# Both products of the delta rule's 64-wide join over all 128 rows, with zeros in the idle half of one factor

## The chip, the cores and the metric

One NeuronCore of a Trainium2 chip runs the kernel. The metric is the device time in microseconds of one execution; the time before the change is the median of three runs.

## The reference

One decoder layer on 256 tokens of width 2048, in float32. The input is projected to the operands of two token mixers, a gated delta rule with 16 heads of 128 and a differential softmax attention with 16 heads; their outputs are gated, merged and projected, and a dense SwiGLU layer follows. What matters here is the delta rule. Each head works in chunks of 64 tokens:

```
k_beta = k * beta
a_mat = jnp.where(strict, jnp.einsum('bhncd,bhnsd->bhncs', k_beta, k) * decay, 0.0)
sol = lax.linalg.triangular_solve(a_mat + jnp.eye(C, dtype=f32), rhs, left_side=True,
                                  lower=True, unit_diagonal=True)
```

The kernel does not solve this way. It treats 128 tokens at a time as one unit, two chunks of 64 with the passage between them kept in the same 128 by 128 matrix, builds the inverse of the unit lower triangle, and multiplies by it.

## The kernel before, in words

**The work.** Everything hangs on one stream of weight tiles of 256 by 512 (in DRAM in the order of use), each 512 KB. SyncE's queue brings them into a ring of four (`raw`), ScalarE rounds a tile to fp32r (`whi`), VectorE forms the remainder (`wlo`), both three tiles ahead of use, and TensorE takes twelve matmuls of 512 columns per tile: for two blocks of 128 rows of the weights and two of 128 tokens, activation high part by weight high part, high by low, low by high. The result gathers in the PSUM buffers `pg`.

**The slots.** The first five bodies are of 32 slots each, one weight tile per slot (`BODY`, `TPG`). Each engine's program walks the slots and calls, after the tile of a slot, functions with an `if s == ...` that put in a piece of the mixers. So the order of the small work within each engine is written out by hand, by slot numbers, and engines meet through counting semaphores. In body j (0 to 3) `dn_conv` and `dn_build` prepare four heads of the delta rule; `dn_scan` in body j + 1 uses what they built.

**The build.** For the four heads there are eight units of 128 tokens (index i, 0 to 7). `AT` holds for each the scaled and masked matrix of key products, 128 by 128. The inverse is built from blocks of 8 (on GpSimd) to 16 to 32 (slots 19 to 23), then the 32-wide blocks are joined to 64 (slots 25 to 27), and the 64-wide ones to 128 in the last slots, called the join here. `T` holds the inverse of the upper 64 rows (its rows 64 to 127 are cleared once at the start and not written again), and `TTf` the whole inverse, transposed, as it grows.

**The join.** In slot 29 (`OFF_64`) TensorE computes for each unit the product of `AT[0:64, i, 64:128]` with `T[0:64, i, :]` (L648 to 651). The results of units 0 to 3 go to PSUM partitions 64 to 127, those of units 4 to 7 to partitions 0 to 63, alternately. ScalarE copies them to `Pm`, units 0 to 3 to its rows from 64 and units 4 to 7 to its rows from 0 (L1058, L1059), and beforehand it has copied the lower right block of `TTf` for units 4 to 7 to rows 0 to 63 (L1056), since both factors of a product must lie in the same rows. In slot 30 TensorE computes the second product for each unit, units 0 to 3 over rows 64 to 127 and units 4 to 7 over rows 0 to 63 (L655 to 658), and ScalarE copies the negated results into the upper right block of `TTf` (L1062, L1063). The reader of the finished `TTf` is the first product of `dn_scan` in slot 1 of the next body (L673).

**Around it.** `S` holds the state of the delta rule after the first half of the tokens. ScalarE writes it in slot 2 of a body (L1106), TensorE reads it in slot 3 (`pe_ks`, L686 to 690), and it is unused until the next body. GpSimd, in each body, steps the blocks of 8, issues four transfers of the first turn (`blocks_in`, L1415), finds the reciprocal root for the key norms and signals `pool_rinv` (L1437, L1438), and then issues the four transfers of the second turn and the four of the values. `dn_scan` on VectorE waits for `pool_rinv` in slot 0 of the next body.

A product in fp32 (`float32` operands) shows as two LDWEIGHTS and two MATMULs in the profile; one of fp32r operands as one of each. `B8`, `B4` and `C8` are views of the PSUM buffers `B`.

Of the kernel before, what the change touches and what calls it, by code (L numbers as in the profile page):

```python
# [106 lines left out]
def build(nc, xT, xrow, weights, w_ab, consts, early, params, lam_in, ln_in, out):  # L107
# [8 lines left out]
    with ctx:  # L116
# [80 lines left out]
        B4 = [b[:, :].rearrange("p (h d) -> p h d", h=HB) for b in B]  # L197
        B8 = [b[:, :].rearrange("p (h d) -> p h d", h=8) for b in B]
        C8 = [b[:, 0:8 * SB].rearrange("p (h d) -> p h d", h=8) for b in B]
        TT, WT = Pm[:, :, 0:SB], Pm[:, :, SB:CH]  # L200
        sel = masks[:, 0, 0:SB // EB]
        eye32 = masks[:, 6, :]
# [34 lines left out]
        def d_(name):  # L237
            a, b = DS[name]
            return dsm[:, a:b]
# [254 lines left out]
        def _(pe):  # L494
            def mm(o, l, r, start=True, stop=True):
                return nc.tensor.matmul(o, l, r, start=start, stop=stop)  # L496
# [110 lines left out]
            def dn_build(j, s):  # L607

                if s == 13:
                    pe.wait_ge(N["act_silu"], 1 + 3 * j + 1)  # L610
                    pe.wait_ge(N["dve_conv"], 1 + 6 * j + 2)
                    pe.wait_ge(N["dve_o1"], 1 + j)
                    for t in range(TOK):
                        for h in range(HB):
                            kc = cT[:, 0, h, t * P:(t + 1) * P]
                            last = mm(B4[2 + t][:, h, :], kc, kc)
                    last.then_inc(N["pe_kk"], 1)
                if s in GROW:
                    k = GROW[s]
                    f0, f1 = SB if k == 0 else 0, SB if k == GROWN - 1 else CH  # L620
                    pe.wait_ge(N["dve_x"], 1 + GROWN * j + k + 1)
                    waits_end()
                    for i in range(8):
                        for q in range(4):
                            a = sub(q)
                            last = mm(B8[1][a, i, f0:f1], (Tc if k == 0 else Pc)[a, i, :], Pm[a, i, f0:f1])
                    last.then_inc(N["pe_x"], 1)
                if s == OFF_P:
                    pe.wait_ge(N["dve_t"], 1 + 2 * j + 1)
                    pe.wait_ge(N["act_at"], 1 + j + 1)  # L630
                    waits_end()
                    for i in range(8):
                        for q in (0, 2):
                            last = mm(C8[2][sub(q + 1), i, :], AT[sub(q), i, sub(q + 1)], Tc[sub(q), i, :])
                    last.then_inc(N["pe_p"], 1)
                if s == OFF_T:
                    pe.wait_ge(N["dve_p"], 1 + j + 1)
                    waits_end()
                    for i in range(8):
                        for q in (0, 2):  # L640
                            b = sub(q + 1)
                            last = mm(C8[1][sub(q), i, :], Pc[b, i, :], TT[b, i, :])
                    last.then_inc(N["pe_t"], 1)
                if s == OFF_64:
                    pe.wait_ge(N["dve_t"], 1 + 2 * (j + 1))
                    pe.wait_ge(N["act_tt"], 1 + j + 1)
                    waits_end()
                    for i in range(HB):  # L648
                        mm(B8[1][CH:P, i, :], AT[0:CH, i, CH:P], T[0:CH, i, :])
                        last = mm(B8[1][0:CH, HB + i, :], AT[0:CH, HB + i, CH:P], T[0:CH, HB + i, :])  # L650
                    last.then_inc(N["pe_p21"], 1)
                if s == OFF_64 + 1:
                    pe.wait_ge(N["act_p21"], 1 + j + 1)
                    waits_end()
                    for i in range(HB):  # L655
                        mm(B8[2][0:CH, i, :], Pm[CH:P, i, :], TTf[CH:P, i, CH:P])
                        last = mm(B8[1][0:CH, i, :], Pm[0:CH, HB + i, :], Pm[0:CH, i, :])
                    last.then_inc(N["pe_x21"], 1)

            def dn_scan(j, s, alone=False):  # L660
# [207 lines left out]
        def _(act):  # L868
            def copy(o, i, scale=1.0):
                return nc.scalar.activation(o, i, ACT.Copy, scale=scale)  # L870
# [153 lines left out]
            def dn_build(j, s):  # L1024
                if s == 2 and not isinstance(j, int):
                    sums_in(j)
                if s in DECAY and not isinstance(j, int):
                    past(j, s - DECAY[0], len(DECAY))
                    if s == DECAY[-1]:
                        decay(j)  # L1030
                if s == 12 and isinstance(j, int):
                    past(j, 0, 1)
                if s == 13 and isinstance(j, int):
                    decay(j)
                if s in AT_SCALED:
                    a = 4 * AT_SCALED.index(s)
                    act.wait_ge(N["dve_ss"], 1 + j + 1)
                    for i in range(a, a + 4):
                        last = nc.scalar.activation(AT[:, i, :], AT[:, i, :], ACT.Copy, scale=d_("e")[:, i:i + 1])
                    if a:  # L1040
                        last.then_inc(N["act_at"], 1)
                if s == 24:
                    silu(j, 1)
                if s == OFF_COPY:
                    act.wait_ge(N["dve_t"], 1 + 2 * j + 1)
                    for q in range(4):
                        a = slice(q * SB, (q + 1) * SB)
                        copy(TTf[a, :, a], TT[a])
                    for q in range(2):
                        a = slice(q * SB, (q + 1) * SB)  # L1050
                        last = copy(T[a, :, a], Tc[a])
                    last.then_inc(N["act_tt"], 1)
                if s == OFF_64:
                    act.wait_ge(N["dve_t"], 1 + 2 * (j + 1))
                    act.wait_ge(N["act_tt"], 1 + j + 1)
                    copy(Pm[0:CH, 0:HB, :], TTf[CH:P, HB:8, CH:P])  # L1056
                    act.wait_ge(N["pe_p21"], 1 + j + 1)
                    copy(Pm[CH:P, 0:HB, :], B8[1][CH:P, 0:HB, :])  # L1058
                    copy(Pm[0:CH, HB:8, :], B8[1][0:CH, HB:8, :]).then_inc(N["act_p21"], 1)  # L1059
                if s == OFF_64 + 1:  # L1060
                    act.wait_ge(N["pe_x21"], 1 + j + 1)
                    copy(TTf[0:CH, 0:HB, CH:P], B8[2][0:CH, 0:HB, :], -1.0)  # L1062
                    copy(TTf[0:CH, HB:8, CH:P], B8[1][0:CH, 0:HB, :], -1.0).then_inc(N["act_x21"], 1)  # L1063

            def blocks_out(scratch, kept):

# [327 lines left out]
        def _(pool):  # L1394
# [5 lines left out]
            def root(o, x):  # L1400

                a = half[:, 0:x.shape[1]]
                for i in range(3):
                    ch(G.tensor_tensor(a, o, o, ALU.mult))  # L1404
                    ch(G.tensor_tensor(a, a, x, ALU.mult))
                    ch(G.tensor_scalar(a, a, -0.5, 1.5, ALU.mult, ALU.add))  # L1406
                    last = G.tensor_tensor(o, a, o, ALU.mult)
                    if i < 2:
                        ch(last)
                return last  # L1410
# [7 lines left out]
            for j in range(NB + 1):  # L1418
                if j > 0:
                    pool.wait_ge(N["dve_qs"], 1 + j)  # L1420
                    root(d_("rs"), d_("qs")).then_inc(N["pool_rs"], 1)
                if j < NB:
                    pool.wait_ge(N["dve_a8"], 1 + j + 1)
                    for k in range(EB - 1):
                        col, row, part, rest = below(k)
                        ch(G.tensor_tensor(part, col, row, ALU.mult))  # L1426
                        last = G.tensor_tensor(rest, rest, part, ALU.subtract)  # L1427
                        if k < EB - 2:
                            ch(last)
                    last.then_inc(N["pool_t8"], 1)  # L1430
                    for i in range(2):
                        pool.wait_ge(c_kept, 16 * (2 * j + i + 1))
                        pool.wait_ge(N["dve_raw"], 1 + 2 * j + i)
                        blocks_in(turn_c, moved, c_full)
                        if i == 0:
                            pool.wait_ge(N["dve_ss"], 1 + j + 1)
                            ch(root(d_("rk"), d_("ss")))  # L1437
                            G.tensor_tensor(d_("rinv"), d_("rk"), d_("ss"), ALU.mult).then_inc(N["pool_rinv"], 1)  # L1438
                    pool.wait_ge(v_kept, 16 * (j + 1))
                    pool.wait_ge(N["dve_ktail"], 1 + j + 1)  # L1440
                    blocks_in(turn_v, vtok, v_full)
# [847 lines left out]
```

## Time and profile before the change

| what | value |
| --- | --- |
| median of 3 runs | 1893.19 us (1892.96 to 1893.9) |
| the profiled execution | 1893.05 us |
| its span, first to last instruction | 1891.0 us |
| mean granted TensorE clock | 0.998 of full |
| TensorE busy | 1875.3 us, 99% |
| VectorE, ScalarE, GpSimd busy | 1322.6, 919.5, 200.4 us |
| DMA | 389.70 MB, 206 GB/s on average |

The profile is of one execution. Times of its rows count from the start of the span. A timeline row gives the start, the time from the first start to the last end, the engine, the line of the kernel, the operation, the tiles written and read, the rows and columns of the stationary factor ("64\*64"), the shape and type streamed, and how many instructions were merged into the row; PEld is TensorE's weight load, which overlaps its matmuls.

### The profile page before, as it was taken

How to read it: one execution, taken by the hardware profiler on the slowest of the kernel's cores; microseconds unless marked ns; L12 is line 12 of the kernel's file. 1: busy time of each engine (PE TensorE's matmuls, PEld its weight loads, DVE VectorE, ACT ScalarE, POOL GpSimd, SP SyncE). 2: the span in 40 equal slices, each digit the busy share in tenths (PEclk: the TensorE clock that was granted, in tenths of full speed). 3: DMA queues.
4: the chain of work that ended last, by engine and by line, in shares of the span. 5: the costliest groups of instructions: out<-in, count | busy, mean ns of one | idle time of the engine just before them, and what ended most of it. 6: DMA issues, size and time to landing. Idle time of an engine off the chain costs nothing.

```text
span 1891.0 us, 29975 instructions
## 1 busy us (share of the span) xinstructions
PE 1875.3 (99%) x9647; PEld 1548.5 (82%) x9647; DVE 1322.6 (70%) x1859; ACT 919.5 (49%) x1234; POOL 200.4 (11%) x480
## 2 busy tenths in 40 slices
PE   9999999999999999999999999999999999999997
PEld 7788888878888888888888888888888888888886
DVE  7888889897666767675577657577765466654656
ACT  5655565664454545556444437444443444443442
POOL 0303022030023232333000000000000000000000
PEclk9999999999999999999999999999999999999999
DMA  7667667584567676766666775556655566665565
GB/s 273 214 200 221 213 209 226 184 250 159 190 197 245 215 243 218 246 214 212 200 197 192 231 244 168 200 189 196 192 193 197 190 192 196 191 197 191 190 191 176
DMA packets 117970, 389.70 MB, mean 206 GB/s; under 512 B 14512, under 2 KB 23536, under 8 KB 117744
## 3 DMA queue, kind: packets, MB, share of 16 engines
q1 hardware_dynamic: 97904, 351.65, 57.8%
q10 hardware_dynamic: 14592, 24.14, 4.0%
q0 software_dynamic: 5376, 12.59, 2.5%
q8 instruction: 63, 1.03, 0.2%
q14 instruction: 35, 0.29, 0.0%
HBM read 368.91 MB, written 19.42 MB: 205 GB/s over the span
## 4 chain that ended last, share of the span: by engine, by line
PE 96%; DVE 1%; DMA 1%; POOL 0%; issue 0%; ACT 0%; SPq 0%; DVEq 0%; ACTq 0%; POOLq 0%
PE pg L496 91%; PE B L496 5%; DVE gates L1474 1%; DMA raw<-in_weights 0%; POOL Tc L1427 0%; DMA qT<-turn_c 0%; PE B L596 0%; POOL Tc L1426 0%; PE B L816 0%; ACT whi L870 0%; DVE act_b L1466 0%; DVE wlo L1466 0%; POOL qT L1415 0%; PE B L744 0%; DVE lnst L2170 0%
## 5 line engine op out<-in xcount | busy, mean ns | idle before, releaser
L1466 DVE TENSOR_TENSOR wlo<-raw,whi 128x1024 fp32r<-128x1024 f32 (+1 forms) x640 | 778.5, 1219 | 468.0 <-ACT whi L870 448.9
L870 ACT ACTIVATE whi<-raw 128x1024 fp32r<-128x1024 f32 (+1 forms) x640 | 673.8, 1057 | 747.7 <-PE pg L496 715.7
L496 PE MATMUL pg<-whi,act_x 128*128 128x512 f32 x2960 | 936.0, 393 | 1.8 <-ACT whi L870 1.8
L496 PEld LDWEIGHTS pg<-whi,act_x 128*128 128x128 f32 x2960 | 555.3, 188 | 120.5 <-ACT whi L870 2.2
L496 PE MATMUL pg<-wlo,act_x 128*128 128x512 f32 x1480 | 574.6, 390 | 0.0
L496 PE MATMUL pg<-whi,act_a 128*128 128x512 f32 x1632 | 504.6, 389 | 0.0
L496 PEld LDWEIGHTS pg<-whi,act_a 128*128 128x128 f32 x1632 | 306.3, 188 | 63.8 <-DVE act_a L1466 0.2
L496 PEld LDWEIGHTS pg<-wlo,act_x 128*128 128x128 f32 x1480 | 278.1, 188 | 55.0
L496 PE MATMUL pg<-wlo,act_a 128*128 128x512 f32 x816 | 317.5, 389 | 0.0
L496 PEld LDWEIGHTS pg<-wlo,act_a 128*128 128x128 f32 x816 | 153.2, 188 | 31.7
L496 PE MATMUL pg<-whi,act_b 128*128 128x512 f32 x512 | 158.5, 389 | 0.0
L496 PEld LDWEIGHTS pg<-whi,act_b 128*128 128x128 f32 x512 | 96.1, 188 | 19.9
L496 PE MATMUL pg<-wlo,act_b 128*128 128x512 f32 x256 | 99.6, 389 | 0.0
L1931 DVE STREAM_TRANSPOSE soft<-hraw 32x256 f32<-32x256 f32 x208 | 90.6, 436 | 3.8
L496 PEld LDWEIGHTS pg<-wlo,act_b 128*128 128x128 f32 x256 | 48.0, 188 | 10.0
L1474 DVE SCALAR_TENSOR_TENSOR cT<-vda,cw,cT 128x255 f32<-128x255 f32 (+2 forms) x96 | 41.8, 477 | 1.1
L1177 ACT ACTIVATE soft<-soft,sm 128x128 f32<-128x128 f32 (+1 forms) x64 | 28.3, 445 | 15.3 <-DVE sm L1470 15.3
L1415 POOL DMA_DIRECT2D gates<-turn_p x48 | 26.1, 550 | 38.0 <-DMA turn_p<-gates 38.0
L1426 POOL TENSOR_TENSOR Tc<-Tc 128x7 f32<-128x7 f32 (+3 forms) x28 | 16.1, 576 | 130.6 <-DVE Tc L1664 128.7
L1406 POOL TENSOR_SCALAR half<-half 128x2 f32<-128x2 f32 (+1 forms) x72 | 24.3, 337 | 6.4
L1474 DVE SCALAR_TENSOR_TENSOR soft<-cst,sm,B 128x384 f32<-128x384 f32 x32 | 18.2, 609 | 9.0 <-PE B L496 7.6
L1404 POOL TENSOR_TENSOR half<-dsm 128x8 f32<-128x8 f32 x24 | 6.3, 263 | 168.7 <-DVE dsm L1471 167.4
(265 smaller groups left out, 1086.6 us busy)
## 6 DMA issues: line engine op xcount, KB each, us to landing
raw<-in_weights SPq DMA_DIRECT2D x646, 512.0 KB, 4.2
turn_c<-hraw ACTq DMA_DIRECT2D x8, 512.0 KB, 3.2
qT<-turn_c POOLq DMA_DIRECT2D x32, 128.0 KB, 3.3
turn_q<-hraw ACTq DMA_DIRECT2D x6, 512.0 KB, 3.7
gates<-turn_q ACTq DMA_DIRECT2D x24, 128.0 KB, 5.0
turn_p<-gates POOLq DMA_DIRECT2D x12, 192.0 KB, 3.8
gates<-turn_p POOLq DMA_DIRECT2D x48, 48.0 KB, 4.0
decm<-sums_out ACTq DMA_DIRECT2D x4, 512.0 KB, 3.6
```

Source lines behind the costliest of these rows:

```text
L496: return nc.tensor.matmul(o, l, r, start=start, stop=stop)
L870: return nc.scalar.activation(o, i, ACT.Copy, scale=scale)
L1177: last = nc.scalar.activation(pr[:, m, a:b], pr[:, m, a:b], ACT.Exp, bias=sm[:, 28 + i:29 + i], accum_out=sm[:, 32 + i:33 + i])
L1404: ch(G.tensor_tensor(a, o, o, ALU.mult))
L1406: ch(G.tensor_scalar(a, a, -0.5, 1.5, ALU.mult, ALU.add))
L1415: pool.dma_start(dst[b * SB:(b + 1) * SB], scratch[:, :, b].rearrange("a x (q i) -> x a q i", i=SB)).then_inc(full, 16)
L1426: ch(G.tensor_tensor(part, col, row, ALU.mult))
L1466: return V.tensor_tensor(o, a, b, op)
L1474: return V.scalar_tensor_tensor(out=o, in0=a, scalar=s, in1=b, op0=op0, op1=op1)
L1931: ins = V.transpose(blocks_out(turned)[b * SB:(b + 1) * SB, :, :, a, :], blocks_in[a * SB:(a + 1) * SB, :, :, b, :])
```

## The change

All eight products of each place run over rows 0 to 127. In the first, both factors are taken whole: rows 64 to 127 of `T` are zero. All results land in PSUM partitions 64 to 127. ScalarE copies them in one instruction to rows 64 to 127 of `joined`, a view of `S` as eight blocks of 64; rows 0 to 63 of it are cleared by GpSimd in every body, in front of the operation that signals `pool_rinv`, once the readers of `S` are done. In the second product `joined` with its zero rows is multiplied by all rows of the right half of `TTf`, the results land in partitions 0 to 63, and one ScalarE copy negates them into `TTf`. The copy of the lower right block to `Pm` is gone, and ScalarE waits for `pool_rinv` before it writes `joined`.

```diff
@@ -197,6 +197,7 @@
         C8 = [b[:, 0:8 * SB].rearrange("p (h d) -> p h d", h=8) for b in B]
+        joined = S[:, :, :].rearrange("p h (e d) -> p (h e) d", d=CH)
@@ -645,16 +646,14 @@
                     pe.wait_ge(N["dve_t"], 1 + 2 * (j + 1))
                     pe.wait_ge(N["act_tt"], 1 + j + 1)
                     waits_end()
-                    for i in range(HB):
-                        mm(B8[1][CH:P, i, :], AT[0:CH, i, CH:P], T[0:CH, i, :])
-                        last = mm(B8[1][0:CH, HB + i, :], AT[0:CH, HB + i, CH:P], T[0:CH, HB + i, :])
+                    for i in range(8):
+                        last = mm(B8[1][CH:P, i, :], AT[:, i, CH:P], T[:, i, :])
                     last.then_inc(N["pe_p21"], 1)
                 if s == OFF_64 + 1:
                     pe.wait_ge(N["act_p21"], 1 + j + 1)
                     waits_end()
-                    for i in range(HB):
-                        mm(B8[2][0:CH, i, :], Pm[CH:P, i, :], TTf[CH:P, i, CH:P])
-                        last = mm(B8[1][0:CH, i, :], Pm[0:CH, HB + i, :], Pm[0:CH, i, :])
+                    for i in range(8):
+                        last = mm(B8[2][0:CH, i, :], joined[:, i, :], TTf[:, i, CH:P])
                     last.then_inc(N["pe_x21"], 1)
@@ -1053,14 +1052,12 @@
                 if s == OFF_64:
                     act.wait_ge(N["dve_t"], 1 + 2 * (j + 1))
                     act.wait_ge(N["act_tt"], 1 + j + 1)
-                    copy(Pm[0:CH, 0:HB, :], TTf[CH:P, HB:8, CH:P])
+                    act.wait_ge(N["pool_rinv"], 1 + j + 1)
                     act.wait_ge(N["pe_p21"], 1 + j + 1)
-                    copy(Pm[CH:P, 0:HB, :], B8[1][CH:P, 0:HB, :])
-                    copy(Pm[0:CH, HB:8, :], B8[1][0:CH, HB:8, :]).then_inc(N["act_p21"], 1)
+                    copy(joined[CH:P, :, :], B8[1][CH:P, :, :]).then_inc(N["act_p21"], 1)
                 if s == OFF_64 + 1:
                     act.wait_ge(N["pe_x21"], 1 + j + 1)
-                    copy(TTf[0:CH, 0:HB, CH:P], B8[2][0:CH, 0:HB, :], -1.0)
-                    copy(TTf[0:CH, HB:8, CH:P], B8[1][0:CH, 0:HB, :], -1.0).then_inc(N["act_x21"], 1)
+                    copy(TTf[0:CH, :, CH:P], B8[2][0:CH, :, :], -1.0).then_inc(N["act_x21"], 1)
@@ -1435,6 +1432,9 @@
                             pool.wait_ge(N["dve_ss"], 1 + j + 1)
                             ch(root(d_("rk"), d_("ss")))
+                            if j:
+                                pool.wait_ge(N["pe_ks"], 1 + j)
+                            ch(G.memset(S[0:CH, :, :], 0.0))
                             G.tensor_tensor(d_("rinv"), d_("rk"), d_("ss"), ALU.mult).then_inc(N["pool_rinv"], 1)
```

## Rows read from the trace of the kernel before

**Rows 1.** The page, busy time of each engine with its share and instructions.

```profile
PE 1875.3 (99%) x9647; PEld 1548.5 (82%) x9647; DVE 1322.6 (70%) x1859; ACT 919.5 (49%) x1234; POOL 200.4 (11%) x480
```

**Rows 2.** The page, the chain that ended last, by engine.

```profile
PE 96%; DVE 1%; DMA 1%; POOL 0%; issue 0%; ACT 0%; SPq 0%; DVEq 0%; ACTq 0%; POOLq 0%
```

**Rows 3.** Waits of TensorE from 40 to 500 us: total, times, longest.

```profile
PE B L496 <- DVE Pc L1466: 1.2, 1, 1.2
```

**Rows 4.** Timeline of TensorE around an fp32 product of 128 by 128, first body on.

```profile
117.74 0.39 PE L496 MATMUL pg<-whi,act_x 128*128 128x512 f32 x1
117.96 1.05 PE L496 MATMUL B<-vr,TTf 128*128 128x128 f32 x8
118.77 0.48 PE L496 MATMUL pg<-whi,act_x 128*128 128x512 f32 x1
119.09 0.40 PE L496 MATMUL pg<-wlo,act_x 128*128 128x512 f32 x1
```

**Rows 5.** Timeline of TensorE around the first join product, first body.

```profile
103.38 0.39 PE L496 MATMUL pg<-whi,act_x 128*128 128x512 f32 x1
103.69 0.68 PE L496 MATMUL B<-T,AT 64*64 64x64 f32 x16
104.31 0.50 PE L496 MATMUL pg<-whi,act_x 128*128 128x512 f32 x1
104.64 0.39 PE L496 MATMUL pg<-wlo,act_x 128*128 128x512 f32 x1
```

**Rows 6.** Timeline of TensorE around the second join product, first body.

```profile
106.94 0.39 PE L496 MATMUL pg<-whi,act_x 128*128 128x512 f32 x1
107.25 0.27 PE L496 MATMUL B<-TTf,Pm 64*64 64x64 f32 x1
107.26 0.27 PE L496 MATMUL B<-Pm 64*64 64x64 f32 x1
107.36 0.22 PE L496 MATMUL B<-TTf,Pm 64*64 64x64 f32 x1
...
107.71 0.22 PE L496 MATMUL B<-TTf,Pm 64*64 64x64 f32 x1
107.72 0.22 PE L496 MATMUL B<-Pm 64*64 64x64 f32 x1
107.87 0.50 PE L496 MATMUL pg<-whi,act_x 128*128 128x512 f32 x1
```

**Rows 7.** Timeline of the weight loads there, first and last of one tile's eight.

```profile
107.25 0.13 PEld L496 LDWEIGHTS B<-TTf,Pm 64*64 64x64 f32 x1 [0.35 <-issue]
...
107.66 0.14 PEld L496 LDWEIGHTS B<-TTf,Pm 64*64 64x64 f32 x1
```

**Rows 8.** Timeline of TensorE at the attention's score products.

```profile
523.36 0.39 PE L496 MATMUL pg<-whi,act_x 128*128 128x512 f32 x1
523.67 1.58 PE L496 MATMUL B<-kT,qT 64*128 64x128 f32 x16
```

**Rows 9.** Timeline of TensorE at the second half of the beta and a projections.

```profile
23.08 0.39 PE L496 MATMUL pg<-whi,act_x 128*128 128x512 f32 x1
23.30 1.99 PE L496 MATMUL B<-act_x,act_a 128*64 128x256 f32 x16
25.12 0.40 PE L496 MATMUL pg<-whi,act_x 128*128 128x512 f32 x1
```

**Rows 10.** Timeline of ScalarE around the join, first body.

```profile
104.14 0.41 ACT L870 ACTIVATE Pm<-TTf 64x256 f32<-64x256 f32 x1
104.57 0.77 ACT L870 ACTIVATE Pm<-B 64x256 f32<-64x256 f32 x2
105.37 1.06 ACT L870 ACTIVATE whi<-raw 128x1024 fp32r<-128x1024 f32 x1
```

**Rows 11.** Timeline of GpSimd, first body.

```profile
81.40 0.20 POOL L1438 TENSOR_TENSOR dsm<-dsm 128x8 f32<-128x8 f32 x1
89.81 2.21 POOL L1415 DMA_DIRECT2D qT<-turn_c  x4 [8.21 <-DMA turn_c<-hraw]
```

**Rows 12.** Instructions that touch the tile T: VectorE's clear, ns min/median/max.

```profile
L1498 DVE MEMSET T<- x1: 485/485/485, 2.0 to 2.0; 128x512 f32 x1
```

## The prediction

> **What bounds the kernel now.** I read the page first. TensorE is busy for 99% of the span and ends 96% of the chain of waits [rows 1, 2]; no other engine passes 70%. So time added to TensorE's own stream is added to the run, and time saved on ScalarE is worth nothing unless TensorE waits for it. Inside the delta rule TensorE's waits have one entry for VectorE that matters below: 1.2 us, once, for the operand of a growth step in the first body [rows 3].
>
> Next the timeline of TensorE around the two places that the change touches. Between two weight products of 512 columns the start-to-start gap is 0.22 to 0.23 us (117.74 to 117.96 in [rows 4]). The first join product is 16 recorded matmuls (each fp32 product shows as two): the last wide product before it starts at 103.38, the first small one at 103.69, the next wide ones at 104.31 and 104.64 [rows 5]. From wide start to the second wide start behind it that is 1.26 us, of which two ordinary gaps (0.46) would be there anyway. The parts are 0.31 in, 0.46 from first to last small start (0.68 less the 0.22 that the last one lasts), 0.15 out, 0.33 to the next. The second product is the same: 106.94 is its wide start and 107.87 the next, and here the trace lists the matmuls one by one [rows 6]. The reader is to see that they start in pairs 0.01 us apart, one from each of the two 64-row, 64-column tiles, and that a tile starts its next only 0.058 us later ((107.71-107.36)/6), the first step being 0.11. The loads of one tile keep the same step: (107.66-107.25)/7 = 0.059 us [rows 7]. So the 0.46 us for 16 is not 0.03 each: it is eight steps of a tile, with two tiles side by side.
>
> **The change, part by part.** There are four bodies and two places in each, so everything on TensorE counts eight times.
>
> Number of instructions: eight products per place before, eight after; 16 recorded loads and 16 matmuls either way. Loaded columns (64) and moving columns (64) do not change.
>
> What changes is the side by side. All eight products of a place now use all 128 rows and write the same 64 output partitions, so there is one tile and nobody to pair with. Sixteen steps of one tile: 0.11 + 14 x 0.058 = 0.92 us from first to last start, against 0.46. That the longer column of rows costs nothing by itself is seen in the wide fp32 products: 8 matmuls, 128 rows, take 1.05 us, so (1.05-0.27)/7 = 0.111 each for 128 loaded columns [rows 4], almost exactly twice the 0.058 for 64. The step follows the columns, not the rows. I take 0.058; the lower bound is the 0.031 per matmul of today's pairs (0.46/15), the upper one is in the second rival.
>
> Entry and exit. The products of 128 by 128 are entered after 0.22 us and left after 118.77 - 118.74 = 0.03, then 0.32 [rows 4]. The 64 by 64 ones pay 0.31, 0.15 and 0.33 [rows 5], and so do the score products of 64 rows by 128 columns, 0.31 on entry [rows 8]. The difference, 0.09 + 0.12 + 0.01 = 0.22 us, is paid for each detour out of the full array. Does a product of 128 rows by 64 columns pay it? One stage has that shape, the beta and a projections: entry 0.22, exit 25.12 - 25.01 = 0.11, which is its own step of (1.99-0.28)/15 = 0.114, so nothing is paid [rows 9]. But that stage multiplies fp32r operands into partitions from 0, as one matmul per product; the join is fp32 at two matmuls per product, and its first product goes to partitions from 64. Every fp32 stage with fewer than 128 rows pays; no fp32 one with 64 columns and 128 rows exists here. So one row is nearest by shape and the others by type and by how many matmuls a product takes. I take the detour as still paid (0.22 us kept), because the small fp32 tiles pay it in both shapes shown; the other end is 0.22 us gained per place. The Trainium skill, "TensorEngine Tiling (Array Packing)", sections Available Configurations and Key Properties, lists 128 by 64 as a mode of its own and says that a change of mode drains the engine: by that rule the detour stays and the sum is the one below; by the projection rows alone it would be the first rival's.
>
> Per place: +0.46 us. Eight places: +3.7 us.
>
> ScalarE loses a copy at the first place (0.41 us) and replaces two of 64 by 256 (0.77 us together) with one of 64 by 512 [rows 10]; two of half its width take 0.77 together, so one takes no more. I cost it at nothing: the copy behind the first product ended at 105.34 and the second product starts at 107.25, a cover of 1.9 us, and a first product that ends 0.46 us later still leaves 1.4 us. Without that cover each 0.1 us would be four tenths over the run. Behind the ScalarE waits stands the rounding of the next weight tile at 105.37; it starts some 0.3 us later (0.46 later product, less what the single copy saves), and TensorE wants that tile only three tiles on, at 12 x 0.23 = 2.7 us each, with VectorE's subtraction between. The new wait of ScalarE for the pool's inverse is met long before: the pool finishes it at 81.6 in the first body [rows 11] and ScalarE asks at 104. The result copy at the second place ends 0.4 us later; its reader comes at 117.96 [rows 4].
>
> GpSimd clears 64 rows of S in front of that inverse and waits for the state products of the body before, which lie at its beginning, over 50 us back. Queued behind the clear are the inverse and the four transfers of the second turn, issued from 89.81; between 81.6 and 89.81 the pool is idle [rows 11], 8.2 us of cover. No row shows a pool clear of this size. VectorE's clear of T, 512 elements per partition, took 0.485 us [rows 12]; I take the pool's as 0.5 to 1.0 us, hidden. What it could do is hold up VectorE in the first body, where TensorE is already waiting for VectorE [rows 3]: nothing at the low end, its own length of 1.0 us once at the high end. I take 0, since it starts at about 81.4, when the product whose result that growth step needs is not yet being worked on by VectorE.
>
> **The sum.** The profiled execution took 1893.05 us for a span of 1891.0. 1893.05 + 8 x 0.46 = 1896.73; it stands 0.14 below the median of the three runs, so against that the forecast is 1893.19 + 3.7 = 1896.9 us.
>
> **The rivals.** *No detour:* the 128-row shape is run as part of the full array. Then 0.22 + 15 x 0.058 + 0.03 + 0.32 = 1.44 us per place against 1.26, +0.18, times eight +1.45: 1894.6 us. For it the projection rows [rows 9]; against it that they are of another type and go to the lower partitions. Chance 0.18.
>
> *Load and stream in turn:* with one set of rows in use, a load can't run under the matmul before. The step is then 0.058 for the load plus 0.055 for the stream (128 streamed columns fit into a step of 0.111 [rows 4], so 64 take at most half), 0.113 us; 15 x 0.113 - 0.46 = +1.24 per place, +9.9 in all: 1903.1 us, slower beyond doubt. It decides as soon as the step passes 0.059. Against it: the wide fp32 products hide a 128-column load under a 128-column stream on the same rows, at 0.111. The Trainium skill, "TensorE: Matmul & The Clock Gate", section Part 3, has this rule (a load overlaps a running matmul only where the row group differs); the wide rows speak against it. Chance 0.07.
>
> *Not slower at all:* the full array takes the products with neither detour nor loss of the side by side, at 0.031 per matmul: 0.22 + 0.46 + 0.03 + 0.32 = 1.03 us per place, -0.23, in all -1.8: 1891.4 us. It decides if the 0.058 step belongs to the two-tile mode and not to 64 loaded columns; against it stands 0.111 for 128. Chance 0.05.
>
> **How the numbers follow.** The forecast case has 0.70. A measurement of this kernel can tell about 0.2%, 3.8 us, from no change, and +3.7 lies just under that: half of this case falls on either side, and the pool's clear can only push it up. So slower by over 0.2% is 0.35 + 0.07 = 0.42, within 0.2% is 0.35 + 0.18 + 0.03 = 0.56, faster 0.02. The range goes down to the first rival less a few tenths (1894.2) and up to the forecast with 1.0 us for the clear and some tenths of step (1898.6); in-turn loading and the gain are left out.
>
> **What would show it.** In the changed profile both places list 16 matmuls of 128 by 64 columns in about 1.14 us (0.92 + 0.22) where 0.68 stood, 0.31 after the last wide start, and the next wide one 0.15 after the last small start. The first rival shows 0.22 and 0.03 to 0.11 there; the second about 1.95 us for the sixteen. A TensorE wait over 1.2 us in the first body would be the clear's. Wrong I would be most simply if the step of one tile with 128 rows is not 0.058.

## The result, and the profile after

The changed kernel takes 1897.32 us (median of 20 runs), the kernel before, run beside it, 1893.82 us (20 runs): 3.5 us more. The ratio is 1.0017, 95% interval 1.0011 to 1.0024, so +2.1 to +4.5 us. One run of the kernel before took 2349.5 us, far over 1.5% above its fastest, and is left out of the ratio as a slow one. The forecast was +3.7 us, 1896.9 us.

The page after, the lines that answer to [rows 1, 2]: busy times, and the chain that ended last.

```profile
PE 1880.0 (99%) x9647; PEld 1553.2 (82%) x9647; DVE 1322.9 (70%) x1859; ACT 916.9 (48%) x1222; POOL 203.2 (11%) x484
...
PE 95%; DVE 2%; DMA 1%; ACT 1%; issue 1%; POOL 0%; SPq 0%; DVEq 0%; ACTq 0%; POOLq 0%
```

The same number of matmuls and loads (9647 each) keeps TensorE busy 4.7 us longer. ScalarE has 12 instructions fewer and 2.6 us less to do, which bought nothing: TensorE still sets the end.

The timeline of TensorE around the first place, first body, the answer to [rows 5]:

```profile
103.82 0.39 PE L497 MATMUL pg<-whi,act_x 128*128 128x512 f32 x1
104.14 1.15 PE L497 MATMUL B<-T,AT 128*64 128x64 f32 x16
105.21 0.50 PE L497 MATMUL pg<-whi,act_x 128*128 128x512 f32 x1
105.55 0.39 PE L497 MATMUL pg<-wlo,act_x 128*128 128x512 f32 x1
```

and around the second, the answer to [rows 6]; here all sixteen are one form and stand in one row:

```profile
107.84 0.39 PE L497 MATMUL pg<-whi,act_x 128*128 128x512 f32 x1
108.16 1.15 PE L497 MATMUL B<-TTf,S 128*64 128x64 f32 x16
109.23 0.50 PE L497 MATMUL pg<-whi,act_x 128*128 128x512 f32 x1
109.57 0.39 PE L497 MATMUL pg<-wlo,act_x 128*128 128x512 f32 x1
```

The sixteen matmuls take 1.15 us where they took 0.68. Entry is 104.14 - 103.82 = 0.32, the next gap 0.34: as before within 0.01. From wide start to second wide start it is 105.55 - 103.82 = 1.73 us against 1.26, and 109.57 - 107.84 = 1.73 at the second place. The other three bodies show the same gaps within 0.01. In the trace's single records the difference is 0.46 at each place: 8 x 0.46 = 3.7 us.

The weight loads of the first place, the answer to [rows 7]:

```profile
104.14 1.01 PEld L497 LDWEIGHTS B<-T,AT 128*64 128x64 f32 x16 [0.35 <-issue]
```

Sixteen loads start over about 0.87 us (1.01 less the 0.14 that one lasts), 0.058 apart, while each matmul is recorded as lasting 0.22. So each load is recorded under matmuls of the same rows. The ends of matmuls are modelled in this profile; a reading that rests on starts alone stands at the full array below.

ScalarE and GpSimd, from their timelines, the answers to [rows 10, 11]:

```profile
105.40 0.60 ACT L869 ACTIVATE S<-B 64x512 f32<-64x512 f32 x1 [0.82 <-PE B L497]
106.02 1.06 ACT L869 ACTIVATE whi<-raw 128x1024 fp32r<-128x1024 f32 x1
```

```profile
80.65 0.52 POOL L1437 MEMSET S<- 64x512 f32 x1
81.25 0.20 POOL L1438 TENSOR_TENSOR dsm<-dsm 128x8 f32<-128x8 f32 x1
90.28 2.22 POOL L1412 DMA_DIRECT2D qT<-turn_c  x4 [8.82 <-DMA turn_c<-hraw]
```

The copy ends at 106.00 and the second product starts at 108.16, 2.2 us of cover. The clear takes 0.52 us and the pool is idle for 8.8 us behind it.

The two profiled executions lie 1897.35 - 1893.05 = 4.3 us apart, 0.6 more than the eight places. Matched weight product by weight product, the two traces move apart by 0.46 us at each of the eight places, 3.70 in all, and otherwise in four stretches only: the changed kernel is 0.73 us ahead after the first 21 us, then loses 0.87 where TensorE stopped once, 0.30 at the wait for the growth step [rows 3], and 0.2 near 1161 us. So the 0.6 is a sum of several differences of these two executions, and one of them alone, the stop, is larger than it. The stop lies in the middle of a growth step of the first body, among products that all stand behind one and the same wait. In its timeline:

```profile
78.82 0.97 PE L497 MATMUL B<-Pm,Pc 32*32 32x64 f32 x52
80.37 0.41 PE L497 MATMUL B<-Pm,Pc 32*32 32x64 f32 x12 [0.58 <-issue]
```

The executions profiled of four of the variants below (two column tiles, no clear, first place only, by twos) do not have this gap, and it is not in the profile of the kernel before. What caused it no run shows.

### The profile page after: what moved, and what is told of

It is laid out like the page before. It is cut to its first block, busy times and chain, and to the rows that moved or that the text cites. A ratio compares the mean times of both kernels' runs of the same rounds, so it can differ in the third digit from the quotient of the medians.

```text
span 1895.3 us, 29974 instructions
## 1 busy us (share of the span) xinstructions
PE 1880.0 (99%) x9647; PEld 1553.2 (82%) x9647; DVE 1322.9 (70%) x1859; ACT 916.9 (48%) x1222; POOL 203.2 (11%) x484
## 4 chain that ended last, share of the span: by engine, by line
PE 95%; DVE 2%; DMA 1%; ACT 1%; issue 1%; POOL 0%; SPq 0%; DVEq 0%; ACTq 0%; POOLq 0%
PE pg L497 90%; PE B L497 5%; DVE gates L1474 1%; DMA raw<-in_weights 1%; ACT whi L869 0%; DMA qT<-turn_c 0%; POOL Tc L1424 0%; DVE wlo L1466 0%; DVE act_b L1466 0%; PE B L597 0%; POOL Tc L1423 0%; DVE sm L1474 0%; ACT gates L1295 0%; POOL qT L1412 0%; PE B L815 0%
## 5 line engine op out<-in xcount | busy, mean ns | idle before, releaser
L997 ACT ACTIVATE cT<-vda,cw 128x256 f32<-128x256 f32 x32 | 14.4, 497 | 21.4 <-DVE vda L1602 21.4
```

The lines of the kernel that those rows point to most:

```text
L997: last = nc.scalar.activation(cT[:, kind, h, :], conv_in(kind, h), ACT.Copy, scale=cw[:, kind, h, CONV - 1:CONV])
```

## The experiments

All are compared with the kernel before on the same chip. A "place" is one of the two products of the join; its length is taken from the wide start ahead of it to the second wide start behind it: 1.26 us before, 1.73 after.

**Two column tiles over 128 rows.** The changed kernel, with the units split over both halves of the output partitions:

```diff
-                    for i in range(8):
-                        last = mm(B8[1][CH:P, i, :], AT[:, i, CH:P], T[:, i, :])
+                    for i in range(HB):
+                        mm(B8[1][CH:P, i, :], AT[:, i, CH:P], T[:, i, :])
+                        last = mm(B8[1][0:CH, HB + i, :], AT[:, HB + i, CH:P], T[:, HB + i, :])
```

and the same at the second place.

> The changed kernel, all products still over 128 rows, but units 0 to 3 and 4 to 7 write opposite halves of the output partitions, alternately, in both places; the ScalarE copies are two of 64x256 again. Theory (what was lost is the side by side of two tiles, rows cost nothing): each place goes from 1.15 us for its 16 matmuls back to about 0.68, entry 0.31 and exit 0.15 stay; 8 x 0.46 = 3.7 us less than the changed kernel, the time of the kernel before within 0.5 us. Rival (128 rows exclude any pairing, both column halves wait for the same row streams): the 16 stay at 1.15 us and the kernel at +3.5 us over before.

Measured 1893.71 us against 1893.84, ratio 0.9997 (0.9988 to 1.0006). Its first place in the timeline of TensorE:

```profile
104.09 0.39 PE L497 MATMUL pg<-whi,act_x 128*128 128x512 f32 x1
104.41 0.69 PE L497 MATMUL B<-T,AT 128*64 128x64 f32 x16
105.02 0.50 PE L497 MATMUL pg<-whi,act_x 128*128 128x512 f32 x1
105.36 0.39 PE L497 MATMUL pg<-wlo,act_x 128*128 128x512 f32 x1
```

These are 128 rows, zeros and all, and the place takes 1.27 us as in the kernel before. The whole loss is in how many tiles the products are spread over; the rows, the clear and the state buffer cost nothing that can be seen. The rival falls.

**First place in the full array.** The changed kernel, with all 128 columns of `AT` loaded and 128 output partitions written:

```diff
-                        last = mm(B8[1][CH:P, i, :], AT[:, i, CH:P], T[:, i, :])
+                        last = mm(B8[1][:, i, :], AT[:, i, :], T[:, i, :])
```

> The changed kernel with the first place in the full array: all 128 columns of AT loaded, 128 output partitions, of which ScalarE copies the wanted half as before. Theory (any output narrower than 128 pays the detour; the step follows the loaded columns): entry 0.23 and exit 0.03 instead of 0.32 and 0.15, step 0.111, so 0.23 + 15 x 0.111 + 0.35 = 2.24 us from wide start to second wide start, against 1.72 in the changed kernel: +0.5 us in each of four bodies, +2.1 us over the changed kernel. Rival (the step is set by the 64 streamed columns, not the loaded ones): step 0.058, 1.45 us, so 1.1 us less than the changed kernel.

Measured 1899.5 us against 1893.84, ratio 1.0027 (1.0017 to 1.0037). In the timeline of TensorE:

```profile
105.24 0.39 PE L497 MATMUL pg<-whi,act_x 128*128 128x512 f32 x1
105.47 1.89 PE L497 MATMUL B<-T,AT 128*128 128x64 f32 x16
107.17 0.48 PE L497 MATMUL pg<-whi,act_x 128*128 128x512 f32 x1
107.49 0.39 PE L497 MATMUL pg<-wlo,act_x 128*128 128x512 f32 x1
```

Entry is 0.23 instead of 0.32: the detour is gone. The mean step is (1.89-0.27)/15 = 0.108 us with 64 streamed columns. The single records, merged in this row, start 0.055 us apart once and then every 0.111 to 0.112, which is the step of the products with 128 loaded and 128 streamed columns [rows 4]. So the step follows the loaded columns, and half the streamed ones take nothing off it. The place takes 107.49 - 105.24 = 2.25 us, as expected, though with an exit of about 0.08 instead of 0.03 and a first step shorter by about as much. Against the changed kernel's 1.73 that is 0.52 more, the balance of two prices: avoiding the detour is worth 0.2 us a place, and doubling the loaded columns costs 0.7.

**First place only.** The kernel before, with the 128-row product at the first place and its own second place.

```diff
+                    for i in range(8):
+                        last = mm(B8[1][CH:P, i, :], AT[:, i, CH:P], T[:, i, :])
...
+                    copy(Pm[0:CH, HB:8, :], B8[1][CH:P, HB:8, :]).then_inc(N["act_p21"], 1)
```

> The kernel before with only the first place of the change (all 128 rows, one tile); ScalarE copies the results of units 4 to 7 from the upper output partitions to rows 0 to 63 of Pm, and the second place, S and the clear stay as before. Theory (each place costs 0.46 by itself): +1.8 us over the kernel before; 16 matmuls in 1.15 us at the first place, 0.68 at the second. Rival (a part of the loss comes from ScalarE, GpSimd or the second place alone): under 1.4 us or over 2.3.

Measured 1895.72 us against 1893.67, ratio 1.0012 (1.0002 to 1.0021): +2.1 us. Its interval would bear +0.4 to +4.0; the trace is sharper:

```profile
104.10 0.39 PE L496 MATMUL pg<-whi,act_x 128*128 128x512 f32 x1
104.41 1.15 PE L496 MATMUL B<-T,AT 128*64 128x64 f32 x16
105.49 0.50 PE L496 MATMUL pg<-whi,act_x 128*128 128x512 f32 x1
105.82 0.39 PE L496 MATMUL pg<-wlo,act_x 128*128 128x512 f32 x1
```

The place takes 1.72 us with none of the change's other parts present, and the unchanged second place takes 1.27. The two places add up.

**No clear.**

```diff
-                            if j:
-                                pool.wait_ge(N["pe_ks"], 1 + j)
-                            ch(G.memset(S[0:CH, :, :], 0.0))
...
             V.memset(T[:, :, :], 0.0)
+            V.memset(S[:, :, :], 0.0)
```

> The changed kernel without GpSimd's clear of rows 0 to 63 of S and its wait in each body; S is cleared once at the start by VectorE. So in bodies 1 to 3 the second product also adds rows 0 to 63 of the old state times rows of TTf. Theory (the clear is hidden): the time of the changed kernel within 0.4 us, and the places look the same. Rival (the clear holds up the first body's growth chain, 1.5 us of TensorE wait there against 1.2 before): 0.3 to 0.9 us less.

Measured 1897.27 us against 1893.84, ratio 1.0018 (1.0009 to 1.0027), and the changed kernel's own median is 1897.32. These times alone could not tell the 0.3 to 0.9 us of the rival from nothing. TensorE's wait for the growth step [rows 3] decides. In the changed kernel, with two column tiles (which keeps the clear) and without the clear it is, in this order:

```profile
PE B L497 <- DVE Pc L1466: 1.5, 1, 1.5
PE B L497 <- DVE Pc L1470: 1.3, 1, 1.3
PE B L497 <- DVE Pc L1463: 1.3, 1, 1.3
```

With the clear it is 1.3 or 1.5 us, without it 1.3, and in the first-place-only variant, which has no clear either, 1.3. So nothing of the time can be laid on the clear: it is hidden.

**Not interleaved.** The kernel before, with units 0 to 3 first and 4 to 7 behind them:

```diff
                     for i in range(HB):
                         mm(B8[1][CH:P, i, :], AT[0:CH, i, CH:P], T[0:CH, i, :])
+                    for i in range(HB):
                         last = mm(B8[1][0:CH, HB + i, :], AT[0:CH, HB + i, CH:P], T[0:CH, HB + i, :])
```

> The kernel before, only the order of the eight products in each place changed: units 0 to 3 first, then 4 to 7, so that neighbours in the queue share a tile. Theory (two tiles overlap only for neighbours in the order of issue): each block of four products takes 8 steps of 0.058 by itself, the 16 take about 1.1 us instead of 0.68, and the kernel is as slow as the changed one, about +3.5 us. Rival (TensorE reaches past waiting instructions to the other tile): 0.68 us stays and the time is that of before.

Measured 1896.48 us against 1893.84, ratio 1.0014 (1.0005 to 1.0024). The timeline of TensorE at its second place, where the two tiles have different names:

```profile
108.91 0.50 PE L496 MATMUL B<-TTf,Pm 64*64 64x64 f32 x5
109.20 0.27 PE L496 MATMUL B<-Pm 64*64 64x64 f32 x1
109.25 0.22 PE L496 MATMUL B<-TTf,Pm 64*64 64x64 f32 x1
109.31 0.22 PE L496 MATMUL B<-Pm 64*64 64x64 f32 x1
...
109.37 0.22 PE L496 MATMUL B<-TTf,Pm 64*64 64x64 f32 x1
109.42 0.45 PE L496 MATMUL B<-Pm 64*64 64x64 f32 x5
109.80 0.50 PE L496 MATMUL pg<-whi,act_x 128*128 128x512 f32 x1
```

It is slower, as the theory said, but by less: 2.6 us, of which the places explain 8 x 0.28 = 2.2. The second tile starts at 109.20, when the first has started five of its eight. From first to last start it is 0.74 us, neither 0.92 (one tile after the other) nor 0.46 (side by side). So my "only neighbours" was wrong: TensorE reaches past three waiting matmuls of the first tile; with four waiting the second tile had not started. It is not that matmuls can't be handed over faster, since with four tiles (below) all sixteen start within 0.25 us.

**By twos.** To see whether that reach is enough for short runs, the order was two products of one tile, then two of the other:

```diff
+                    for i in range(0, HB, 2):
+                        for k in range(i, i + 2):
+                            mm(B8[1][CH:P, k, :], AT[0:CH, k, CH:P], T[0:CH, k, :])
+                        for k in range(i, i + 2):
+                            last = mm(B8[1][0:CH, HB + k, :], AT[0:CH, HB + k, CH:P], T[0:CH, HB + k, :])
```

> The kernel before with the products of each place in the order of two of one tile, two of the other. In the not interleaved order the second tile started while the first still had 3 or 4 of its 8 matmuls to start, so TensorE does reach past waiting ones, but not far. Theory (it reaches past about four matmuls): four of one tile hide in that reach, and the 16 start within 0.46 to 0.52 us, as when they alternate. Rival (only neighbours overlap): about 0.8 us.

One run took 1892.9 us, which alone says little. The trace does:

```profile
103.10 0.73 PE L496 MATMUL B<-T,AT 64*64 64x64 f32 x16
```

It is 0.73 - 0.22 = 0.51 us from first to last start, 0.05 more than when the products alternate. The reach covers it.

**Four tiles at the second place.** If tiles are what counts, four should beat two. The units in rows 0 to 63 and those in rows 64 to 127 are each split over the lower and upper output partitions:

```diff
+                    for i in range(2):
+                        mm(B8[2][0:CH, i, :], Pm[CH:P, i, :], TTf[CH:P, i, CH:P])
+                        mm(B8[1][0:CH, i, :], Pm[0:CH, HB + i, :], Pm[0:CH, i, :])
+                        mm(B8[2][CH:P, 2 + i, :], Pm[CH:P, 2 + i, :], TTf[CH:P, 2 + i, CH:P])
+                        last = mm(B8[1][CH:P, 2 + i, :], Pm[0:CH, HB + 2 + i, :], Pm[0:CH, 2 + i, :])
```

> The kernel before with only the second place changed: units 2, 3 and 6, 7 write the upper output partitions, so the eight products lie in all four 64x64 tiles, taken in turn; ScalarE copies four pieces of 64x128. Theory (a step of 0.058 belongs to a tile, tiles run side by side if neighbours in the queue): four steps in each tile, the 16 matmuls start within 0.107 + 2 x 0.058 + 0.02 = 0.24 us instead of 0.46; -0.22 us in each of four bodies, -0.9 us against the kernel before. Rival (at most two tiles at a time): 0.46 stays and the time is that of before.

Measured 1893.43 us against 1893.67, ratio 0.9997 (0.9988 to 1.0006); 0.9 us is too little for these runs. The trace shows the first four at 106.92, 106.93, 106.94 and 106.94 and the next round 0.11 later, as expected; the place takes 107.65 - 106.60 = 1.05 us against 1.26. The rival of two at a time falls.

```profile
106.60 0.39 PE L496 MATMUL pg<-whi,act_x 128*128 128x512 f32 x1
106.92 0.27 PE L496 MATMUL B<-TTf,Pm 64*64 64x64 f32 x1
106.93 0.27 PE L496 MATMUL B<-Pm 64*64 64x64 f32 x1
106.94 0.27 PE L496 MATMUL B<-TTf,Pm 64*64 64x64 f32 x1
106.94 0.27 PE L496 MATMUL B<-Pm 64*64 64x64 f32 x1
107.03 0.22 PE L496 MATMUL B<-TTf,Pm 64*64 64x64 f32 x1
...
107.17 0.22 PE L496 MATMUL B<-Pm 64*64 64x64 f32 x1
107.31 0.50 PE L496 MATMUL pg<-whi,act_x 128*128 128x512 f32 x1
107.65 0.39 PE L496 MATMUL pg<-wlo,act_x 128*128 128x512 f32 x1
```

**Four tiles at both places.** For the first, half the units' factors have to lie in rows 64 to 127:

```diff
+                if s == 22:
+                    act.wait_ge(N["act_at"], 1 + j + 1)
+                    copy(AT[CH:P, HB:8, 0:CH], AT[0:CH, HB:8, CH:P])
...
-                        last = copy(T[a, :, a], Tc[a])
+                        copy(T[a, 0:HB, a], Tc[a, 0:HB])
+                        last = copy(T[CH + q * SB:CH + (q + 1) * SB, HB:8, a], Tc[a, HB:8])
...
+                    V.transpose(T[CH + SB:P, HB:8, 0:SB], TTf[0:SB, HB:8, SB:CH]).then_inc(N["dve_t"], 1)
```

> The kernel before with both places in four 64x64 tiles. For the first, T keeps units 4 to 7 in rows 64 to 127 (ScalarE and VectorE write them there), and ScalarE copies the upper right block of AT of these units to the lower left in slot 22. Theory: 0.24 instead of 0.46 us at eight places, -1.8 us against the kernel before, about 1892.0. Rival (the added ScalarE copies, some 1.5 us per body, or the VectorE transpose make TensorE wait): no gain, and TensorE's waits in the bodies grow.

Measured 1891.95 us against 1893.67, ratio 0.9992 (0.9983 to 1.0001), an interval that still reaches past 1.

> The same kernel as with four tiles in both places, timed again, since 1.7 us is at the edge of what one series can tell. Theory (the trace's 0.22 us at eight places is all there is): again 1.2 to 2.4 us under the kernel before. Rival (its median was luck): within 0.5 us of the kernel before.

The second series measured 1891.43 us against 1893.85, ratio 0.9987 (0.9978 to 0.9996), below 1 throughout. The timeline of TensorE at the first place and of ScalarE behind it, from the first series:

```profile
103.23 0.39 PE L496 MATMUL pg<-whi,act_x 128*128 128x512 f32 x1
103.55 0.46 PE L496 MATMUL B<-T,AT 64*64 64x64 f32 x16
103.94 0.50 PE L496 MATMUL pg<-whi,act_x 128*128 128x512 f32 x1
104.28 0.39 PE L496 MATMUL pg<-wlo,act_x 128*128 128x512 f32 x1
```

```profile
105.06 1.12 ACT L874 ACTIVATE Pm<-B 64x128 f32<-64x128 f32 x4
```

Sixteen matmuls take 0.46 us, and the place 1.05. ScalarE now takes 1.12 us for four copies instead of 0.77 for two and is done at 106.18; the second product starts at 106.89, so 0.7 us of cover is left of 1.9. TensorE's wait for the growth step is still 1.2 us in this execution and no new one is listed in the bodies. (The one profiled in the second series took 1897.3 us, the slowest of its eleven, with 3.5 us of TensorE waits for VectorE in the first body; the profile of the not interleaved variant, which adds no work to ScalarE or VectorE, has 3.2 us of the same waits there. So they are not a mark of the added copies; why some executions have them no run shows.) 8 x 0.22 = 1.8 us is what the medians show, 1.7 and 2.4. This is the fastest of the versions run, and 5 to 6 us under the changed one, each taken against the kernel before.

## Why the prediction was right

**Side by side (the step that carries the sum).** The sixteen matmuls of one tile were put at 0.92 us from first to last start; the profile after gives 1.15 - 0.22 = 0.93. That the step belongs to the tile and not to the rows was read from pairs of starts 0.01 apart [rows 6] and from 0.111 for 128 columns [rows 4]; the two column tiles over 128 rows show it directly. One thing no run separates: the products of one tile here also write the same partitions of the same PSUM buffer. Either alone does not hold pairs apart, since the kernel before pairs products into one buffer at its first place and into the same partitions of two buffers at its second.

**The detour.** It was taken as kept, because the smaller fp32 tiles paid it, against the one row of the same shape [rows 9]; that was a judgement between unlike rows, not a reading, and it came true. After the change the entry is 0.32 at both places, also where the output starts at partition 0. So it is not the upper half that makes it: the fp32 products of 128 rows and 64 columns paid it, and those of 128 rows and 128 columns did not. The Trainium skill, "TensorEngine Tiling (Array Packing)", section Key Properties, says that a change of tiling mode drains the engine. The trace of the two places agrees (0.32 in, against 0.23 in the full array), the projections do not (0.22 in for 128 by 64 [rows 9]). Besides them the kernel before has one more narrow product over 128 rows, a transpose by 32 columns at 40.61 us, entered after 0.23 us and left after 0.03. Both of these narrow ones are recorded as one matmul per product, the fp32 ones that paid as two; whether that is the reason no run here shows. The first rival is out.

**Load and stream in turn.** This rival is out: the step is 0.058 us, not 0.113, and in the full array 64 streamed columns take the same 0.111 to 0.112 as 128, where streaming behind the load would have made a difference. The Trainium skill, "TensorE: Matmul & The Clock Gate", section Part 3, lets a load overlap a running matmul only across row groups; this trace does not agree, with loads 0.058 us apart under matmuls of 0.22 on the same 128 rows.

**Not slower at all.** This rival is out too: the step is 0.058, not 0.031. The kernel does run 128-row products 0.031 apart on average when two column tiles share them, so it is the single tile that costs, as the forecast said.

**ScalarE.** Its copy takes 0.60 us where I had bounded it by 0.77, hidden as said. The cover left is 2.2 us where I had 1.4: I took the later end of the first product off it and forgot that the second product starts later by the same 0.46. **GpSimd.** Its clear takes 0.52, at the low end of 0.5 to 1.0, and is hidden, as the waits with and without it say.

**The sum.** The forecast was +3.7; the trace has eight times 0.46, and the medians +3.5. The agreement is closer than the interval of +2.1 to +4.5 can vouch for; the trace, place by place, is what bears it out. All of that interval is above zero, and it lies on both sides of the 3.8 us at which I had divided the forecast case. Three small slips changed nothing in it: the gap read at 117.74 to 117.96 [rows 4] leads to an fp32 product, though two weight products lie 0.23 apart as well (105.55 and 105.78 in the changed kernel); eight starts of a tile are seven steps, not eight; and the in-turn rival's sixteen would take 15 x 0.113 + 0.22 = 1.92 us, not 1.95.

## What to carry to other kernels

Where TensorE is the bound, count the steps of each tile, not the matmuls. With 64 loaded and 64 streamed columns a recorded fp32 matmul costs about 0.058 us in its tile, and products in other tiles, queued within a few of it, start some 0.007 us apart and add next to nothing. With more streamed than loaded columns the stream can set the step instead: among the score products [rows 8], which load 128 columns, the single records of one tile show the next start 0.22 us behind a matmul that streams 256 columns and 0.11 behind one that streams 128 (0.21 behind the first). Filling the idle half of a factor with zeros to make the products alike saves copies on another engine and gives the second tile away, unless the results are spread over both halves of the output partitions. Two tiles to four was worth 0.22 us per place, and leaving the full array at all costs another 0.22.

## What the runs showed of the hardware that I had not expected

Two column tiles under the same 128 rows run fully side by side, as two tiles of 64 rows do in the kernel before (0.69 and 0.68 us for sixteen). TensorE starts products of a free tile past about three waiting matmuls of a busy one: from first to last start it is 0.74 us for two runs of eight recorded matmuls, 0.51 for runs of four, 0.46 alternating. The starts then leave the order of the program: the second tile's first comes before the first tile's last three. And with 128 columns loaded the step stays at 0.111 to 0.112 us although only 64 are streamed.
